# Attention with the values held in TensorE and the transposed probabilities streamed, two query tiles side by side; the spatial product's groups alternate

## The reference

```
sc  = einsum('qd,kd->qk', q, k) * scale + bias
p   = exp(sc - max(sc))
den = sum(p, axis=-1)
o   = einsum('qk,kd->qd', p, v) / den
y_att  = o_att @ w_proj_att
merged = sigmoid(g_att + gb_att) * y_att + sigmoid(g_ssm + gb_ssm) * y_ssm
```

```
sg = einsum('gts,bnsgc->bntgc', w_m, vc) + b_s.T[:, :, None]
```

## Time and profile before

| | before |
|---|---|
| time, median of 3 runs | 2041.53 us (2040.7 to 2043.28) |
| the profiled execution | 2039.93 us, its span 2038.2 us |
| PE busy | 2010.5 us, 99% of the span |
| POOL, DVE, ACT busy | 64%, 53%, 32% |
| attention, first scores to first projection product | 230.72 to 549.29 us |
| spatial product | within 1343.8 to 1414.5 us |

### The profile page before, as it was taken

How to read it: one execution, slowest core, us unless ns; L and a number is a source line. 1 busy time by engine, 2 the same in 40 slices (tenths; PEclk the granted TensorE clock), 3 DMA queues, 4 the chain that set the end, 5 groups by cost and what they waited for, 6 DMA issues and landing times. The chain is left out here.

```text
span 2038.2 us, 25797 instructions
## 1 busy us (share of the span) xinstructions
PE 2010.5 (99%) x10043; PEld 1676.9 (82%) x10043; DVE 1086.4 (53%) x1397; ACT 647.1 (32%) x1068; POOL 1305.1 (64%) x757
## 2 busy tenths in 40 slices
PE   7999999999999999999999999999999999999998
PEld 3788988888888887788888888888888888888888
DVE  7981256555562485665632277731554555535554
ACT  3302232332331264534400035433434433321103
POOL 2538545665255539999944555976787888859750
PEclk9999999999999999999999999999999999999999
DMA  9545546444444204323475240334133322198432
GB/s 372 143 97 165 192 133 182 131 139 150 160 165 159 110 23 143 103 96 132 162 284 194 82 157 22 124 121 128 63 124 129 120 104 89 46 347 303 144 135 83
DMA packets 188360, 293.24 MB, mean 144 GB/s; under 512 B 12920, under 2 KB 136784, under 8 KB 188240
## 3 DMA queue, kind: packets, MB, share of 16 engines
q1 hardware_dynamic: 178256, 268.53, 38.9%
q10 hardware_dynamic: 9984, 23.07, 2.9%
HBM read 211.64 MB, written 79.94 MB: 143 GB/s over the span
## 5 line engine op out<-in xcount | busy, mean ns | idle before, releaser
L964 POOL TENSOR_SCALAR w_h<-raw 128x512 fp32r<-128x512 f32 (+2 forms) x108 | 237.4, 2198 | 334.1 <-issue 144.8
L1511 PE MATMUL ps<-tb,w_h 128*128 128x512 f32 x1344 | 416.7, 391 | 2.6 <-DVE quads L2798 1.9
L1049 POOL TENSOR_TENSOR w_l<-raw,w_h 128x512 fp32r<-128x512 f32 x210 | 308.9, 1480 | 96.9 <-ACT w_h L2068 96.9
L1511 PEld LDWEIGHTS ps<-tb,w_h 128*128 128x128 f32 x1344 | 251.3, 188 | 59.1 <-issue 3.9
L1511 PE MATMUL ps<-tb,w_l 128*128 128x512 f32 x672 | 261.5, 389 | 0.0
L966 POOL TENSOR_TENSOR w_l<-raw,w_h 128x512 fp32r<-128x512 f32 (+2 forms) x108 | 200.3, 1854 | 9.0
L2068 ACT ACTIVATE w_h<-raw 128x512 fp32r<-128x512 f32 x210 | 130.8, 627 | 235.3 <-PE ps L1511 150.3
L1511 PE MATMUL ps<-act_h,w_h 128*128 128x512 f32 x504 | 196.3, 390 | 0.6 <-ACT quads L2097 0.5
L1511 PE MATMUL ps<-act_h,w_l 128*128 128x512 f32 x504 | 196.1, 389 | 0.0
L1511 PE MATMUL ps<-act_l,w_h 128*128 128x512 f32 x504 | 196.1, 389 | 0.0
L1511 PEld LDWEIGHTS ps<-tb,w_l 128*128 128x128 f32 x672 | 126.1, 188 | 26.4
(11 more groups left out here) (414 smaller groups left out, 4610.2 us busy)
## 6 DMA issues: line engine op xcount, KB each, us to landing
raw<-in_w_in SPq DMA_DIRECT2D x44, 1024.0 KB, 5.2
raw<-in_w_up SPq DMA_DIRECT2D x16, 1024.0 KB, 5.2
f_scratch<-r SPq DMA_DIRECT2D x16, 1024.0 KB, 8.1
gates_scratch<-quads SPq DMA_DIRECT2D x24, 512.0 KB, 7.6
r<-gates_scratch SPq DMA_DIRECT2D x12, 1024.0 KB, 6.0
ada_lo<-in_w_ada SPq DMA_DIRECT2D x16, 512.0 KB, 3.6
ada_hi<-in_w_ada SPq DMA_DIRECT2D x16, 512.0 KB, 4.3
gates_scratch<-gate_st ACTq DMA_DIRECT2D x32, 256.0 KB, 2.0
```

The source lines that it names most:

```text
L964: nc.gpsimd.tensor_scalar(w_h[:, k, c, :], src[:, c, :], 1.0, None, ALU.mult).then_inc(s["w_high"], 1)
L1049: nc.gpsimd.tensor_tensor(w7_l[:, SLOTS[o]], x, w7_h[:, SLOTS[o]].bitcast(F32), ALU.subtract)\
L1511: last = nc.tensor.matmul(bank_of(n, bank), w[:, SLOTS[o], c, :], x(c), start=(first and c == 0 and p == 0), stop=(c == KD // 2 - 1 and p ...
```

## The change

- `values` takes two neighbouring query tiles at once. V (128 keys x 64) is stationary, the transposed probabilities (128 columns) are moving; tile 0 of the pair writes output partitions 0 to 63 and tile 1 partitions 64 to 127, in turn per block of keys. The result has head width on partitions and queries on columns, which is how the projection wants it: `out_transposes` is gone.
- The tiles of a head run from 7 down to 0 and no longer alternate; a pair is (7,6), (5,4), (3,2) or (1,0). So an even `t` has no value product at all, and the pair's products stand at odd `t`, ahead of `transposes(t + 1)`.
- Because odd tiles can be long now, the gate's PSUM bank moves from slot 1 to slot 3. The order on ScalarE stays.
- Division by `den` comes later. Its inverse is needed along the columns, so every 4 tiles `over_denominators` takes 4 reciprocals per partition, SP writes them to memory (`rden_scratch`, 512 numbers) and reads them back spread over 64 partitions (`over_den`), and `normalised` multiplies 64x512.
- SP's loads of `ys_h`, `ys_l` stay behind its loop over the tiles, which now ends with the write and the reading back of the last `rden`.
- The first projection block does its two `ys` products first, then its two `o` products.
- `spatial` takes the two groups in turn.

```diff
-        tiles = [(h, qb) for h in range(HEADS) for long in range(QB - 1, QB // 2 - 1, -1) for qb in (long, QB - 1 - long)]
+        tiles = [(h, qb) for h in range(HEADS) for qb in range(QB - 1, -1, -1)]
...
+                if t % 4 == 2:
+                    sp.wait_ge(*beyond(rden_ready, t // 4 + 1))
+                    sp.dma_start(rden_d[t // 4].rearrange("(b p) -> p b", p=P), rden[:, t // 4 % 2, :], allow_slow_non_contiguous=True)                      .then_inc(rden_out[0], 16)
+                if t % 4 == 3:
+                    i = t // 4
+                    sp.wait_ge(*beyond(rden_out, 16 * (i + 1)))
+                    if i:
+                        sp.wait_ge(*beyond(o_norm, i))
+                    sp.dma_start(over_den[head_rows(i // 2), :], rden_d[i].partition_broadcast(HD)).then_inc(rden_in[0], 16)
...
-                        last = nc.tensor.matmul(slot(1)[:, HALF:T], w[:, n % 2, c, P * (j % 2):P * (j % 2) + P], x[:, c, tok],
+                        last = nc.tensor.matmul(slot(3)[:, HALF:T], w[:, n % 2, c, P * (j % 2):P * (j % 2) + P], x[:, c, tok],
...
-                for b in range(qb + 1):
-                    last = nc.tensor.matmul(dst[:, 0:HD], src[:, P * b:P * b + P],
-                                            v_st[:, pair % 2, b, HD * (h % 2):HD * (h % 2) + HD],
-                                            start=(b == 0), stop=(b == qb))
+                for b in range(tiles[2 * u][1] + 1):
+                    for i in range(2):
+                        if b <= tiles[2 * u + i][1]:
+                            last = nc.tensor.matmul(slot(3)[HD * i:HD * i + HD, 0:P],
+                                                    v_st[:, pair % 2, b, head_rows(h)], prob_t_of(2 * u + i)[:, P * b:P * b + P],
+                                                    start=(b == 0), stop=(b == tiles[2 * u + i][1]))
...
             for t in range(NT):
                 if t + 3 < NT:
                     scores(t + 3)
                 if t + 1 < NT - 2:
                     gate_part(t + 1)
+                if t >= NT - 2:
+                    gate_part(t)
+                if t % 2:
+                    values(t // 2)
                 if t + 1 < NT:
                     transposes(t + 1)
-                if t == NT - 3:
-                    pe.wait_ge(s["sm_ready"], AHEAD + NT - 1)
-                    pe.wait_ge(s["o_ready"], AHEAD + 2 * NH)
-                    out_transposes(0, slot(0))
-                if t == NT - 2:
-                    gate_part(NT - 2)
-                values(t)
-            pe.wait_ge(s["ptshort"], NT // 2)
-            out_transposes(1, slot(2))
-            gate_part(NT - 1)
-            pe.wait_ge(s["o_ready"], AHEAD + NT)
-            out_transposes(2, slot(3))
-            pe.wait_ge(s["ot_ready"], 2)
-            out_transposes(3, slot(2))
...
-                for g in range(2):
-                    grp = 2 * c + g
-                    for t in range(QB):
+                for t in range(QB):
+                    for g in range(2):
+                        grp = 2 * c + g
                         last = nc.tensor.matmul(extra_of(n)[HD * g:HD * g + HD, P * t:P * t + P],
                                                 vg[:, t, HD * grp:HD * grp + HD], wst[:, grp, :], start=True, stop=True)
...
+            def over_denominators(i):
+
+                h, lo = i // 2, 0 if i % 2 else QB // 2
+                dve.wait_ge(s["p_ready"], 4 * i + 4)
+                if i >= 2:
+                    dve.wait_ge(*beyond(rden_out, 16 * (i - 1)))
+                v.reciprocal(rden[:, i % 2, :], den[:, h % 2, lo:lo + QB // 2]).then_inc(rden_ready[0], 1)
```

More of the change, by code:

```diff
@@ L282, in build @@
         ada_hi = at("ada_hi", [P, KD // 2, NB], 200 * kib)
[L283 to L292, removed]
+        ada_parts = at("ada_part0", [P, NB], 158 * kib + 512), at("ada_part1", [P, NB], 206 * kib)
+        prob = at("prob", [P, 3, T], 160 * kib)
+        prob_t = at("prob_t", [P, 2, T], 172 * kib)
+        gate_st = at("gate_st", [P, 2, HALF], 180 * kib)
+        o_raw = at("o_raw", [P, KA, T], 184 * kib)
+        over_den = at("over_den", [P, HALF], 204 * kib)
+        neg_max = at("neg_max", [P, 4], 207 * kib)
+        den = at("den", [P, 2, QB], 207 * kib + 32)
+        rden = at("rden", [P, 2, QB // 2], 207 * kib + 96)
         sig = at("sig", [P, 2, T], 176 * kib)
@@ L334, in prob_of, with is_long, longs, shorts @@
         def prob_of(t):
-            return (prob_short if t % 2 else prob_long)[:, t // 2 % 2, :]
+            return prob[:, (t + 2) % 3, :]
         def prob_t_of(t):
-            return pt_short if t % 2 else pt_long
+            return prob_t[:, t % 2, :]
+        def is_long(t):
+            return tiles[t][1] >= 4
+        def longs(t):
+            return sum(is_long(i) for i in range(t + 1))
+        def shorts(t):
+            return t + 1 - longs(t)
+        def head_rows(h):
+            return slice(HD * (h % 2), HD * (h % 2) + HD)
+        def token_half(i):
+            return slice(0, HALF) if i % 2 else slice(HALF, T)
         ps = ctx.enter_context(nc.psum_tensor("ps", [P, 4, T], F32))
@@ L1476, in _ @@
                     elif cg:
-                        pe.wait_ge(s["ot_ready"], KA)
-                    product(slot(2 * cg + 1), (N_PROJ + j) % 2, cg, 2, ys_h, ys_l, kw=KA).then_inc(s["gemm"], 1)
-                    first = s["ot_ready"] if j == 0 and cg == 0 else None
-                    product(slot(2 * cg), (N_PROJ + j) % 2, cg, KA, o_h, o_l, each=first).then_inc(s["gemm"], 1)
+                        pe.wait_ge(s["mod2_ready"], NT // 4)
+                    product(slot(2 * cg + 1), (N_PROJ + j) % 2, cg, 2, ys_h, ys_l, kw=KA)
+                    if j:
+                        product(slot(2 * cg), (N_PROJ + j) % 2, cg, KA, o_h, o_l).then_inc(s["gemm"], 2)
+                if j == 0:
+                    for cg in range(2):
+                        product(slot(2 * cg), N_PROJ % 2, cg, KA, o_h, o_l, each=None if cg else s["ot_ready"]).then_inc(s["gemm"], 2)
             pe.wait_ge(s["proj_read"], AHEAD + KD - 1)
@@ L1969, in gate_logits @@
                     act.wait_ge(s["first_half"], HALF_GATE + j + 1)
-                A.activation(gate_st[:, g % 2, :], slot(1)[:, HALF:T], ACT.Identity, bias=col_a("b_gate", j))\
+                A.activation(gate_st[:, g % 2, :], slot(3)[:, HALF:T], ACT.Identity, bias=col_a("b_gate", j))\
                  .then_inc(s["gate_read"], 1)
@@ new lines, in near_half, with read_values @@
+                v.tensor_copy(prob_t_of(t)[:, 0:HALF], slot(2)[:, 0:HALF]).then_inc(s["ptc0"], 1)
+            def read_values(u):
+                h = tiles[2 * u][0]
+                dve.wait_ge(s["pv"], AHEAD + u + 1)
+                for i in range(2):
+                    qb = tiles[2 * u + i][1]
+                    v.tensor_copy(o_raw[head_rows(h), h // 2, P * qb:P * qb + P],
+                                  slot(3)[HD * i:HD * i + HD, 0:P]).then_inc(s["o_ready"], 1)
+                if u % 2:
+                    lo = 2 * N_ADA_EARLY + 2 * (u // 2)
+                    dve.wait_ge(s["ada_done"], ADA_DONE + u // 2 + 1)
+                    v.tensor_tensor(mod[:, lo:lo + 2], slot(3)[:, P:P + 2], col_a("b_ada", lo, 2), ALU.add)\
+                     .then_inc(s["mod2_ready"], 1)
@@ L2694, in _ @@
                 ada_chunks(t // 4, ((0, 1, 2), (3, 4, 5), (6, 7), ())[t % 4])
-                normalised(t)
-                if t == NT - 3:
-                    o_low(0, slot(0))
-            o_low(1, slot(2))
-            o_low(2, slot(3))
-            o_low(3, slot(2))
+                if t % 4 == 2:
+                    over_denominators(t // 4)
+                if t % 2:
+                    read_values(t // 2)
+                if t + 1 < NT and is_long(t + 1):
+                    near_half(t + 1)
+                if t % 4 == 1 and t >= 4:
+                    normalised(t // 4 - 1)
+                if t >= NT - 2:
+                    o_low(t - (NT - 2))
+            normalised(NT // 4 - 1)
+            for c in range(2, KA):
+                o_low(c)
             for k in range(2):
```

128 lines of the change are left out of this document (59 added, 69 removed).

## The result

| | before | after |
|---|---|---|
| median | 2041.12 us (4 runs) | 2053.91 us (2052.26 to 2055.14, 4 runs) |
| the profiled execution, its span | 2039.93, 2038.2 us | 2053.63, 2051.9 us |
| PE busy | 2010.5 us | 1991.9 us |

The ratio is 1.0057 (95% interval 1.0045 to 1.007): slower, by 12.8 us between the medians, and outside the forecast's range of 2033 to 2050. The direction of the miss is that of the rival "Slower by the end of attention".

A forecast was written before the change was run, and what follows sets the result against it. TensorE was taken as the bound, busy for 99% of the span. Terms of 30.8 us gained and 31.1 lost gave 2040.2 for the profiled execution, 2041.8 us as median, no change (0.48); range 2033 to 2050.

The forecast's parts named there:

- Slower by the end of attention: Rival, chance 0.20: SP waits for a write of 512 single numbers, landing about 6.5 us or more; 2047.5 us.
- value products: Attention: two output halves in turn run side by side, 0.109 us per two records; 59.3 us become 42.9, 16.4 saved.
- ends of clusters: Attention: where scores follow transposes directly, 8 transposes take 0.79 us instead of 0.87, at about 60 tiles; 4.8 us saved.
- wait for the softmax: End of attention: TensorE's wait goes, as a value product now stands there; 0.7 us saved.
- the gate's bank: Attention: TensorE waits at 30 places for ScalarE's gate copy, which value products covered before; 22.7 us lost.
- step 61: Attention: with neither score nor gate part there, tiles 60 and 61 wait for the copy of their transposes; 0.8 us lost.
- wait for `ys`: Ahead of the projection: TensorE waits for the `ys` loads, now behind the last `rden`; 6.2 us lost.
- clock: Behind the wait for `ys`: TensorE's clock most likely falls to half speed; 1.4 us lost.
- spatial product: Four calls of `spatial`: 1.90 us each instead of 3.26, with nothing taking it back; 5.5 us saved.
- The queue of SP: End of attention: `ys` loads wait behind the last `rden` write, landing taken as 2.3 us; 6.2 us of waiting.
- The same two DMAs in the middle of attention cost nothing: `rden` write and read-back within attention: about 14 us from reciprocal to use, 5 us for both DMAs; no loss.
- Slower by the halves: Rival, chance 0.04: the two column groups do not overlap, in value products and spatial product; 2075 us.

The follow-up runs named there:

- e2: Kernel after, with `rden` written in 128 pieces of 16 bytes in place of 512 of 4: 2046.62 us, ratio 1.0018.
- e8: Kernel after, with `rden` written in 256 pieces of 8 bytes: 2048.12 us, ratio 1.0023.
- e4: Kernel after, with ScalarE copying the gate's bank before the transposes of tile t+1: 2054.43 us, ratio 1.0052.
- e12: Kernel after, with `rden` in 16-byte pieces and the gate's bank copied first; `ys` loads stay behind the last `rden`: 2029.95 us, ratio 0.9928.
- e5: Kernel after, with all value products of a pair's first tile before those of the second, not in turn: 2070.06 us, ratio 1.0134.
- e3: Kernel after, with `ys` loaded ahead of the last `rden` write and `rden` written in 128 pieces of 16 bytes: 2036.65 us, ratio 0.997.
- e7: Kernel after, with three edits: `ys` loaded early, `rden` in 16-byte pieces, the gate's bank copied first: 2019.36 us, ratio 0.9887.
- e6: Kernel before, with one edit: the spatial product takes its two groups in turn: 2037.41 us, ratio 0.9971.
- e10: Kernel before, plus 16 writes of 512 numbers of 4 bytes to a scratch buffer, not waited for in attention: 2042.32 us, ratio 0.9997.
- e11: e1 once more, unchanged: 2052.7 us, ratio 1.0042.
- e1: Kernel after, with SP issuing the four `ys` loads ahead of the last write of `rden`: 2052.38 us, ratio 1.0039.

## Why the prediction was wrong, step by step

Terms as the forecast had them, and what the profiles of before and after give, by distances between starts:

| step | forecast | measured |
|---|---|---|
| value products | -16.4 | 8 x (1.89 + 1.46 + 1.02 + 0.58) = 39.6, and 2.6 for going in; 59.9 before: -17.7 |
| ends of clusters | -4.8 | transposes 3.50 us a head, 3.92 before: -3.4 |
| `out_transposes` | -3.4 | -3.4 |
| wait for the softmax | -0.7 | -0.7 |
| the gate's bank | +22.7 | +22.8 |
| step 61 | +0.8 | +0.7 |
| all of attention | -1.8 | -2.0 |
| wait for `ys` | +6.2 | +15.2 |
| clock | +1.4 | +1.6 |
| spatial product | -5.5 | -5.4 |
| elsewhere | 0 | +4.3 |

The last five rows add up to the 13.7 us between the two spans; the rows of attention leave 0.3 us over.

**The step that failed** is in "The queue of SP": "Then the write must land: 512 numbers of 4 bytes, a form that the trace does not have; the nearest rows are 2.0 and 2.9 us, and I take 2.3." It took 8.3. The mechanism was right, the order of the queue, the wait at `y_in` and the fall of the clock behind it; the term was mis-sized. The reciprocal at 545.78 to the first `ys` order at 554.80 is 9.0 us (3.0 forecast), the four loads take 9.5 (7.8), and the reciprocal was 3.3 us ahead of TensorE's need, not 4.6: 9.0 + 9.5 - 3.3 = 15.2, against 6.2, and 6.0 of the 9.0 us between them are the landing. That alone would have made the forecast 2047.8, still inside its range; the rest of the miss is the loads (1.7), the lead (1.3) and "elsewhere" (4.3), which the forecast put at nothing without a reason. The rows taken as nearest are stores to memory too, but of 256 and 128 KB and in larger pieces, and I gave a landing over 6.5 us only 0.20 with the words "only 2 KB in all". e2 and e8, with the same 2 KB in fewer pieces, show that bytes were the wrong measure.

The Trainium skill has the form, in "DMA: Bandwidth & Descriptors", section "Rules for kernel authors": a last dimension that is not contiguous becomes one descriptor per element, and should be rearranged. The trace agrees (8705 more packets under 512 bytes, of which 8192 are the elements), and e2, which is that rearrangement, has 6144 fewer. With the form priced by such a rule, and not only by durations among the rows, the range of that term would have been open upward.

**"The same two DMAs in the middle of attention cost nothing"** held in after for TensorE, but not for the reason given. The 14 us were not cover for 5 us of DMA but nearly used up: 8.7 to 13.4 from write to read-back alone. VectorE waited 19.1 us for `over_den` in attention (6.1 in the second profile of after) and 8.3 behind it. TensorE did not feel it, since the gate's waits slowed it; without them it did (e4), and with the 16-byte write it did not (e12).

**The value products** were side by side as the earlier trace rows said, and at the price charged: 0.109 us for two records and 0.15 a pair inside the cluster, and 0.09 or 0.07 ahead of it (0.32 from the gate's last product instead of 0.23, 0.18 from the last of `ada` instead of 0.11). So the trace goes on disagreeing with the rule on loads in the Trainium skill's "TensorE: Matmul & The Clock Gate", Part 3 (The mechanism): pairs that differ in the column group alone overlap (1.89 us for 30 loads and products), and without the turns they don't (3.04 in e5). The rival "Slower by the halves" is out.

**The gate's bank** was right in place, number (30) and size: at the four places of a head the distances from scores to gate are 1.40, 1.19, 1.40 and 1.28 us, 19.7 us more than before in all, and the gate's products take 3.1 us more. The list of waits shows 15.2 us for it, since it counts only from the end of a record; e3 to e7 gave 17.3 back, with a gap of 0.2 to 0.3 us left at two of the four places. "If the wait for the gate is missing (then 2019)" meets e7's 2019.4, but that is luck: e7 has lost the wait for `ys` and the fall of the clock as well, which in the forecast's terms is 7.6 us less than 2019.

**Elsewhere**, a term that the forecast did not have. 1.8 us lie ahead of attention; 1.6 of them are a stretch of products at half speed from 100 us on (clock 0.56 in 100 to 102, 1.00 before). The profiles of e6 and e10, whose code there is that of before, have it too (0.77 and 0.61 over 98 to 104), and of the 14 profiles 11 do, with the change or without; it goes by execution. 2.5 us lie behind attention, 1.4 of them waits for GpSimd's `w_l` near 1814 and 1890. Of the profiles of the other kernels with the change all but e8's show 0.8 to 2.5 us of these waits, e6's 0.2, and before's and e10's none; why is not settled.

**The clock** behind the wait was taken at 1.4 us and cost 1.6: the first 24 products of the projection take 7.21 us, 5.57 before. The forecast's row had it fall some 4.3 us after the last product; here it fell about 2.0 us after it.

## What to carry to other kernels

Price a DMA by the number and size of its pieces before its bytes: a 2 KB write element by element, 16 times, was worth 8 us as long as only its last landing was waited for by TensorE, and 25 once the pace rose. Where SP waits for a landing, everything behind it in its queue waits too, and a wait that a slower engine hides today is tomorrow's bound, so an edit that shows nothing by itself (e4) may be worth 17 us beside another. And where a form is missing from the trace, give the range to its least favourable property, not to the rows that look nearest.

## What the runs showed of the hardware

- 2 KB from 128 partitions to memory, from order to landing with little beside it: 1.4 us in pieces of 16 bytes (2.3 in e3), 3.0 in pieces of 8, 8.3 in pieces of 4 (8.4 in the second profile). With 2 MB of loads beside it the last took 12.7 us, and 11.5 in e11.
- Of the 8.3 us some 6 lie behind the last piece on record, and for 3 us of them nothing at all moves (DMA share 0.00 over 551 to 554).
- With such writes the DMA engines are busy longer for the same data: over 250 to 530 us 58% in after, 49% in e2, at 149 GB/s in both. And others land late: the gate's stores of 256 KB in 6.7 us (median) instead of 2.0.
- TensorE's granted clock was 1.00 in the first us after its last product at 548.8, 0.70 over 550 to 552 and 0.50 (1.2 GHz) from 552 on; work began again at 564.34, and the clock was 0.53 over 566 to 568 and 1.00 (2.4 GHz) from 568. This cost 1.6 us. It also fell behind single waits of 1.6 and 2.4 us in the middle of attention, with products of `ada` at their end (e1, e11, e4).
- Products of 128x64 by 128 columns in fp32: 16 + 14 records in turn between the column halves take 1.89 us, one half after the other 3.04.
